# Where the tensors stand in on-chip memory: two large buffers allocated first, and a scratch tensor narrowed

## The reference

```python
for l in range(DEPTH):                       # DEPTH = 2
    h = rmsnorm(x, norm_attn[l])
    z = h @ w_in[l]                          # 1024 -> 1888 columns, split among three head groups
    o_a = gqa_axial_mixer(...)               # 8 heads of 64, 2 key/value heads, rotary
    o_b = mla_mixer(...)                     # 4 heads, low-rank queries and keys, rotary part shared
    o_c = diff_alibi_mixer(...)              # 4 heads, difference of two softmax maps, distance bias
    x = x + jnp.concatenate([o_a, o_b, o_c], axis=-1) @ w_out[l]
    h = rmsnorm(x, norm_ffn[l])
    x = x + conv_gated_mlp(h, w_up[l], conv_w[l], conv_b[l], w_down[l])   # D_FF = 2816, width-3 conv
return rmsnorm(x, final_norm)
```

## Time and profile before

| | |
|---|---|
| timed runs | 3408.32 us median of 3 (3407.34 to 3413.12) |
| profiled execution, its own time | 3407.34 us |
| its span, first to last instruction | 3405.5 us |
| instructions | 41293 |
| mean granted TensorE clock | 0.951 of full speed |
| PE busy | 3034.8 us, 89% |
| DVE busy | 2210.5 us, 65% |
| ACT busy | 1399.9 us, 41% |
| POOL busy | 825.5 us, 24% |
| DMA engines, mean busy share | 20.1% |

### The profile page before, as it was taken

One profiled execution on the slowest core, in us unless ns is written; L12 is line 12 of the kernel. 1 busy time (PEld: TensorE's weight loads), 2 busy tenths in 40 slices (PEclk: granted clock), 3 DMA queues, 4 the chain that ended last, 5 costly groups with the idle time before them and its releaser, 6 DMA issues.

```text
span 3405.5 us, 41293 instructions
## 1 busy us (share of the span) xinstructions
PE 3034.8 (89%) x13488; PEld 2378.8 (70%) x13488; DVE 2210.5 (65%) x2575; ACT 1399.9 (41%) x1917; POOL 825.5 (24%) x472
## 2 busy tenths in 40 slices
PE   6888999666899999999889889995669999999996
PEld 5666777444678888888767667763447788888885
DVE  4863877899345656556567378779972556555555
ACT  3214888666232222222222178886643222222213
POOL 3113554653320000000121145555524100000002
PEclk8999999888999999999999999997789999999998
DMA  4323211210212112111133331111121112111112
GB/s 159 87 81 90 53 46 41 56 39 6 99 50 62 50 37 62 37 49 37 37 103 92 89 85 46 41 54 44 28 75 50 58 42 62 37 49 49 50 37 62
DMA packets 233562, 198.55 MB, mean 58 GB/s; under 512 B 49344, under 2 KB 207808, under 8 KB 233408
## 3 DMA queue, kind: packets, MB, share of 16 engines
q1 hardware_dynamic: 233408, 196.66, 20.1%
HBM read 163.07 MB, written 33.55 MB: 58 GB/s over the span
## 4 chain that ended last, share of the span: by engine, by line
PE 63%; DVE 15%; issue 13%; ACT 4%; DMA 2%; POOL 2%; DVEq 1%; ACTq 0%; SPq 0%; POOLq 0%
PE ps L1528 26%; PE ps L1542 13%; PE ps L1319 9%; PE ps L1417 5%; PE ps L1448 4%; DVE ps L1136 2%; DVE ptl L1178 2%; PE ps L1428 2%; PE ps L1429 2%; DVE r L1079 2%; PE ps L1513 1%; ACT prob L861 1%; PE ps L1460 1%; DVE rinv L1153 1%; ACT pth L891 1%
## 5 line engine op out<-in xcount | busy, mean ns | idle before, releaser
L574 POOL TENSOR_TENSOR w0l<-wraw,w0h 128x1024 fp32r<-128x1024 f32 x34 | 89.4, 2634 | 1692.7 <-ACT w0h L754 1692.7
L1448 PEld LDWEIGHTS ps<-cst,prob 128*128 128x128 f32 x2048 | 257.2, 148 | 272.2 <-DVE ptl L1178 141.9
L1448 PE MATMUL ps<-cst,prob 128*128 128x128 f32 x2048 | 336.3, 289 | 120.9 <-DVE ptl L1178 57.7
L1178 DVE TENSOR_TENSOR ptl<-ps,pth 128x512 fp32r<-128x512 f32 x512 | 349.0, 687 | 142.7 <-ACT pth L891 136.9
L1417 PE MATMUL ps<-stack 128*128 128x512 f32 (+1 forms) x1152 | 350.1, 426 | 96.6 <-ACT prob L861 77.0
L861 ACT ACTIVATE prob<-ps,nmx 128x1024 f32<-128x1024 f32 x320 | 356.7, 1115 | 83.7 <-DVE nmx L1140 63.6
L1257 DVE TENSOR_TENSOR xT<-ps,xT 128x512 f32<-128x512 f32 x352 | 242.4, 691 | 226.2 <-PE ps L1542 226.1
L891 ACT ACTIVATE pth<-ps 128x512 fp32r<-128x512 f32 x512 | 298.8, 595 | 192.6 <-PE ps L1448 188.7
L1417 PEld LDWEIGHTS ps<-stack 128*128 128x128 f32 (+1 forms) x1152 | 216.2, 199 | 180.9 <-ACT prob L861 115.4
L1319 PE MATMUL ps<-xgh,w0h 128*128 128x512 f32 x768 | 254.9, 414 | 49.9 <-DVE z L1049 15.1
L1542 PE MATMUL ps<-ah,dnh 128*128 128x512 f32 x704 | 276.3, 393 | 21.0 <-DVE dnl L1250 20.1
(11 more groups left out here) (183 smaller groups left out, 6088.1 us busy)
## 6 DMA issues: line engine op xcount, KB each, us to landing
wraw<-in_w_up SPq DMA_DIRECT2D x88, 512.0 KB, 4.6
draw<-in_w_down SPq DMA_DIRECT2D x22, 1024.0 KB, 5.0
wraw<-in_w_in SPq DMA_DIRECT2D x36, 512.0 KB, 4.5
x_d<-xT SPq DMA_DIRECT2D x2, 4096.0 KB, 15.8
raw<-qa_d SPq DMA_DIRECT2D x32, 256.0 KB, 3.8
raw<-ka_d SPq DMA_DIRECT2D x32, 256.0 KB, 4.2
vraw<-v_d SPq DMA_DIRECT2D x32, 256.0 KB, 3.1
wraw<-in_w_out SPq DMA_DIRECT2D x16, 512.0 KB, 5.0
```

Of the source, the lines that this page charges most:

```text
L1178: dve.tensor_tensor(ptl[:, s % NPT, :], ps[:, 4 + s % 2, :], pth[:, s % NPT, :].bitcast(F32), ALU.subtract).then_inc(pt_lo, 1)
L1448: ins = pe.transpose(ps[:, 4 + s % 2, m * P:(m + 1) * P], prob[:, b, m, s * P:(s + 1) * P], ident)
```

## The change

`xgh` and `xgl` are allocated first, and `small` is 8 columns wide and not 10. Nothing else in the source differs.

```diff
+        xgh, xgl = sb(ctx, "xgh", [P, KT, T], F32R), sb(ctx, "xgl", [P, KT, T], F32R)
         vec, cst = sb(ctx, "vec", [P, VW]), sb(ctx, "cst", [P, CW])
         gain0 = sb(ctx, "gain0", [P, KT])
-        small = sb(ctx, "small", [P, 10])
-
-        xgh, xgl = sb(ctx, "xgh", [P, KT, T], F32R), sb(ctx, "xgl", [P, KT, T], F32R)
+        small = sb(ctx, "small", [P, 8])
```

## The result

The changed kernel took 3433.04 us (median of 6, 3432.55 to 3437.26) against 3409.36 us for the kernel before (median of 6 on the same chip, 3407.34 to 3414.26): a ratio of 1.0070 (95% interval 1.0059 to 1.0081). It is slower by 23.7 us. The forecast was 3408 us, with a range of 3400 to 3415, and gave 10% to a slower kernel, so it was wrong; the time fell between its rivals C and D.

The account below looks back on a forecast made before the run. The prediction took PE, busy for 89% of the span, to bound the kernel, though no engine is full in attention. Its sum was 3407.34 + 0 - 0.3 - 0.3 + 0.98 = 3407.7, so 3408 us, range 3400 to 3415.

Parts of the forecast that it names:

- Rival C: Attention: shared access of DVE and POOL falls otherwise, L1154 slows, time rises 18 us to 3426 us; 6%.
- Rival D: Matmuls with moving `xgh` or `xgl` go from 226.7 to 233 ns, costing 34 us: 3442 us; 4%.
- 0, ends in the rivals: PE's `float32r` matmuls: no change from 226.7 ns each, term 0.
- (c): `xgh`, `xgl` lose the rest by 4096 shared with `w0h`, `w0l`, `xT`; up projection claimed to stay at 226.7 ns.
- Rival A: PE reads `float32r` operands faster on a multiple of 64, 215 ns a matmul, 103 us saved: 3305 us; 4%.
- Rival B: DVE's and ACT's 3.8 us and the DMAs' 3.3 us all come in full: -7.1 us, 3401 us; 8%.
- DVE and ACT: Their operations on the chain: at most 0.4% and 1.3% different by start, ends -3.8 and +3.8 us, taken as -0.3 us.
- DMA: About 33 us of streaming on the chain: a tenth either way, -3.3 to +3.3 us, taken as -0.3 us.
- Registers: Addresses of `vec` inside the loops exceed 65535, computed by DVE's and ACT's sequencers with time to spare: cost 0.

Follow-up runs that it names:

- the second sweep: Matmuls alone, without the kernel: finer distances, narrower weights, 256 moving columns, plain float32; 230.0 to 236.6 ns between rests 8 and 240, plain float32 429 ns a pass.
- the first sweep: Without the kernel: 32 back-to-back float32r matmuls of 512 columns for each of 23 pairs of starts; about 227 to 228 ns at equal rests, up to 238.5 otherwise.
- three sweeps: Matmuls without the kernel: pairs of starts; finer distances, widths and formats; starts alternating between matmuls, the last with 226.7 to 233.5 ns at 512 columns.
- the run with the distance kept: Changed kernel with 32 unused bytes ahead of `xgh`, all large tensors again 32 bytes past a multiple of 64: 3435.89 us, 1.0069 of the kernel before.
- The repaired kernel: Changed kernel with 1152 unused bytes behind `small`, so all tensors behind have the rest of `xgh`: 3409.58 us against 3411.36 for the kernel before, 0.9993.

## Why the prediction was wrong, step by step

*The term that failed is PE's, "0, ends in the rivals".* The runs showed +6.6 ns in its place for each `float32r` matmul that reads `xgh` or `xgl`: 226.7 to 233.3 ns, 24 us over the 38 full steps of the gated layers and 3 in the output projections. I took no change on the word of rows 6, where plain float32 matmuls had 0.43 us with both kinds of start. That pair was in the wrong format: the second sweep has 429 ns for plain float32 at rests 0 and 128 alike, while `float32r` goes from 226.7 to 233.5. The nearest rows were near by line and far by mechanism. Even in the right format the pair would have shown nothing: both read weights in `cst` at rest 160, `rstd` at rest 32 and `cv` at 64, so their distances were 128 and 160 by 256. Neither was 0, and the first sweep has 233.5 and 234.3 ns for these two.

*The argument on (c) was false, and the addresses of the source refute it.* I wrote that the distance between `xgh` and `w0h` takes on many values by 4096 already. It does, but weight slices step by 512 bytes and halves of a tile by 2048, so all of them are 0 by 256. In the trace of before every `float32r` product with 128 weight columns has that distance. The only others are odd heads of the query expansion (`ch` with `wqh`), whose slices of 96 columns put the weights 128 off. There the odd heads have 231 to 233 ns in the mean and the even ones 230 to 231, without the longer distance at each change of the number of rows. With 96 weight columns little of the effect shows, as with 64 and 32 in the second sweep. The right question was which powers of two the stream does vary, and below which it doesn't.

*Rival D was the right mechanism at 4%.* Its spacing was 233 ns, measured 233.3, and that agreement is luck: the 233 came from the score matmuls, whose two operands have the same rest, and which keep their 231 ns in the mean before and after, so another cause is at work in them. Its price of 34 us, all of the chain's share of these lines, was too high: the gated layer and output projections paid 27.2 us and got 2.0 back from the clock. The input projections didn't get longer (254.2 and 251.2 us before, 253.3 and 251.4 after), though PE was busy for about 4.9 us more in the first and 3.2 in the second; L1319 is only 32 and 38% of the chain there. "Above 227 ns (D), which rows 4 would show at once" was the right test.

*Rival A* had the surplus of 32 cycles over 512 columns as its clue. The surplus is there at every good distance, and at 256 and 384 columns too, and starts on multiples of 64 do not take it away. No pair of starts in three sweeps is faster than 226.7 ns.

*Rival B*, all small gains in full for -7.1 us, can't be read from the changed kernel, where the loss covers them. The narrowing alone gained 4.1 and 6.9 us, which is of that size, with DVE and ACT as before.

*Rival C* didn't happen: L1154's mean went from 2375 to 2374 ns, PE's wait for it from 57.4 to 57.9 us.

*DVE and ACT* at -0.3 us: right. 1220 became 1219, `z<-z,ra` at 1225 became 1226, ACT's 1061 became 1060, and 1045 against 1059 stayed with the tensors, whatever their start by 64; its cause isn't the place.

*DMA* at -0.3 us, with an end of -3.3, was too small if the narrowing's gain is the transfers': single transfers of short rows gain 0.1 to 0.2 us, a weight tile in the kernel 0.3 to 0.4, and the narrowing alone gave 4.1 and 6.9 us in two series. That the whole of it comes from the transfers is argued from their landing times, not shown: the run with the distance kept saw 1 us for the same starts. The repaired kernel, whose weight tiles start at rest 128, lies between: they land in 4.5 and 4.2 us, and its gain of 1.8 us is inside the noise. The comparison that I used for it, `vec` against `cst`, was of two transfers in different company: `vec` itself went from 3.0 to 2.5 us without changing its rest.

*Registers* at 0: right as far as it shows; DVE and ACT in the gated layer wait as before for PE.

## What to carry to other kernels

Where `float32r` matmuls of 512 columns run back to back, each with its own load of 128 weight columns, the starts of the moving operand and of the weights should be equal by 256 bytes: 226.7 ns a matmul, and 229 to 238 at the other distances tried. In this kernel, where PE is busy for 89% of the span, a shift of one against the other by 64, 96 or 128 bytes cost 0.4%, 1.0% and 0.7%, and the spacing of starts in the profile shows it in one line. When bounding a cost from the nearest row, ask first whether that row has the same format and has ever varied the quantity in question. And a faster or slower stream can move the clock: here the slower one shortened a wait, and PE kept its full clock behind it.

## What the runs showed of the hardware that I had not expected

- The distance effect: for `float32r` with 512 moving columns, 226.7 ns at a distance of 0 by 256, 229.3 at 64, 233.5 at 128, 238.5 at 4; at 128 strictly 229 and 238 in turn.
- It is absent at 256 moving columns (120.0 ns at both) and in plain float32 (429 ns a pass at both), and narrower weights don't make a matmul faster: 230.0 ns with 64 columns at rest 0, where 128 columns have 226.7.
- A part of the loss comes back through the clock: after a wait of 2.28 us PE's clock was at 1.2 GHz for part of the next step, which took 23.64 us; after one of 1.65 us it stayed at 2.4 GHz and the step took 22.66 us, though each matmul in it was slower.
- Writing rows of 512 bytes to a start on a multiple of 256 lands a 512 KB transfer in 3.7 us, others in 3.8 to 3.9.
